# Column sums of the modulation vectors: from four 128x128 TensorE transposes per group to VectorE block transposes and four small products per stage

## The reference, cut to what matters

```python
c_act = jax.nn.silu(c)                                  # (1, 1024)
for l in range(DEPTH):                                  # 2 layers
    mod = c_act @ w_ada[l] + b_ada[l]                   # (1, 6144), w_ada[l]: 1024 x 6144
    sh1, sc1, g1, sh2, sc2, g2 = jnp.split(mod, N_MOD, axis=-1)
    h = modulate(rmsnorm(x, norm1[l]), sh1, sc1)
    ...
    x = x + g1[:, None, :] * (merged @ w_out[l])
    h2 = modulate(rmsnorm(x, norm2[l]), sh2, sc2)
    ...
    x = x + g2[:, None, :] * ((jax.nn.silu(gate) * up) @ w_ffn_out[l])
```

## Time and profile before

| | |
|---|---|
| median of three executions | 1434.57 us (1430.73 to 1435.50) |
| the profiled execution | 1434.96 us, its span 1433.1 us |
| TensorE busy / weight loads | 98% / 92% of the span |
| VectorE busy | 80% |
| ScalarE busy | 58% |
| DMA queue of the weights | 71.0% of 16 engines |
| chain that ended last | TensorE 77%, VectorE 11%, ScalarE 6%, issue 3%, DMA 2% |

### The profile page before, as it was taken

How to read it: one execution, slowest core, us unless ns; L and a number is a source line. 1 busy time by engine, 2 the same in 40 slices (tenths; PEclk the granted TensorE clock), 3 DMA queues, 4 the chain that set the end, 5 groups by cost and what they waited for, 6 DMA issues and landing times.

```text
span 1433.1 us, 25543 instructions
## 1 busy us (share of the span) xinstructions
PE 1407.3 (98%) x10339; PEld 1312.1 (92%) x10339; DVE 1145.7 (80%) x1799; ACT 828.5 (58%) x1249; POOL 10.5 (1%) x21
## 2 busy tenths in 40 slices
PE   8999999999999999999999999999999999999997
PEld 7898888889888888889999999998899999999986
DVE  7898888889798888887778777777777787778763
ACT  6776776445776875343666555444446575554542
POOL 2000000000000000000000000000000000000000
PEclk9999999999999999999999999999999999999999
DMA  9643999985445999987854578798787556778662
GB/s 257 161 140 92 284 266 268 299 229 163 137 140 169 278 259 295 284 248 217 226 153 144 172 233 233 212 250 231 225 235 217 148 147 180 231 208 232 180 186 64
DMA packets 485364, 297.13 MB, mean 207 GB/s; under 512 B 14956, under 2 KB 455792, under 8 KB 485120
## 3 DMA queue, kind: packets, MB, share of 16 engines
q1 hardware_dynamic: 483728, 292.00, 71.0%
q0 software_dynamic: 704, 1.66, 0.4%
q10 hardware_dynamic: 816, 1.84, 0.3%
HBM read 289.43 MB, written 1.05 MB: 203 GB/s over the span
## 4 chain that ended last, share of the span: by engine, by line
PE 77%; DVE 11%; ACT 6%; issue 3%; DMA 2%; SPq 1%; DVEq 0%; ACTq 0%
PE acc L1928 12%; PE acc L1929 12%; PE acc L1930 12%; PE mx L1945 9%; PE acc L1945 8%; PE mx L1946 5%; DVE w_lo L1073 4%; PE acc L1946 4%; DVE ada_acc L1163 2%; ACT w_hi L577 2%; PE acc L1960 1%; PE acc L1961 1%; PE acc L1962 1%; DMA rotb<-projb 1%; PE mx L2363 1%
## 5 line engine op out<-in xcount | busy, mean ns | idle before, releaser
L1073 DVE TENSOR_TENSOR w_lo<-raw,w_hi 128x1024 fp32r<-128x1024 f32 x450 | 541.5, 1220 | 113.3 <-ACT w_hi L577 111.4
L577 ACT ACTIVATE w_hi<-raw 128x1024 fp32r<-128x1024 f32 x450 | 458.2, 1049 | 137.7 <-DMA raw<-in_w_in 83.5
L1928 PE MATMUL acc<-h,w_hi 128*128 128x258 f32 (+1 forms) x1776 | 508.6, 286 | 8.4 <-DVE projb L1591 3.4
L1929 PE MATMUL acc<-h,w_hi 128*128 128x258 f32 (+1 forms) x1776 | 503.7, 284 | 0.0
L1930 PE MATMUL acc<-h,w_lo 128*128 128x258 f32 (+1 forms) x1776 | 498.0, 280 | 0.0
L1928 PEld LDWEIGHTS acc<-h,w_hi 128*128 128x128 f32 x1776 | 335.0, 189 | 15.7 <-issue 4.8
L1930 PEld LDWEIGHTS acc<-h,w_lo 128*128 128x128 f32 x1776 | 338.3, 190 | 0.0
L1929 PEld LDWEIGHTS acc<-h,w_hi 128*128 128x128 f32 x1776 | 335.9, 189 | 2.6 <-issue 2.4
L1945 PE MATMUL mx<-u,w_hi 128*128 128x512 f32 x864 | 303.4, 396 | 0.1
L1946 PE MATMUL mx<-u,w_lo 128*128 128x256 f32 x864 | 240.8, 279 | 0.0
L1945 PEld LDWEIGHTS mx<-u,w_hi 128*128 128x128 f32 x864 | 162.0, 188 | 37.1 <-DVE u L1877 0.4
(11 more groups left out here) (294 smaller groups left out, 1649.1 us busy)
## 6 DMA issues: line engine op xcount, KB each, us to landing
raw<-in_w_in SPq DMA_DIRECT2D x132, 512.0 KB, 4.0
ada<-in_w_ada SPq DMA_DIRECT2D x96, 512.0 KB, 5.0
raw<-in_w_ffn_in SPq DMA_DIRECT2D x88, 512.0 KB, 4.9
raw<-in_w_up SPq DMA_DIRECT2D x64, 512.0 KB, 5.6
raw<-in_w_down SPq DMA_DIRECT2D x64, 512.0 KB, 5.9
raw<-in_w_out SPq DMA_DIRECT2D x32, 512.0 KB, 3.9
raw<-in_w_ffn_out SPq DMA_DIRECT2D x32, 512.0 KB, 4.2
raw<-in_w_ret_o SPq DMA_DIRECT2D x16, 512.0 KB, 3.8
```

The lines of the kernel that those rows point to most:

```text
L577: nc.scalar.activation(w_hi[:, n % NS], raw[:, n % NS], ACT.Copy).then_inc(hi_ready, 1)
L1073: V.tensor_tensor(w_lo[:, n % NS], raw[:, n % NS], w_hi[:, n % NS].bitcast(F32), ALU.subtract).then_inc(lo_ready, 1)
L1928: mm(outp, w_hi[:, i % NS, k], rhs[:, k, 0], start=k == 0, stop=False)
L1929: mm(outp, w_hi[:, i % NS, k], rhs[:, k, 1], start=False, stop=False)
```

## The change

For a group, directly after its eighth product, VectorE now turns `ada_acc` in blocks of 32x32 (`V.transpose`, 128x512 to 128x512) and sums each of the sixteen blocks along its rows into 16 columns of `ada_rows`. Block `(q, b)` of the turned tile holds column `32*b + j` in partition `32*q + j`, summed over the 32 partitions of quarter `q`. What is left is a sum over the four quarters. For it, TensorE does four small float32 products once per stage, after the stage's last group: a 128x32 matrix of four stacked identities (`ada_fold`) times four to 28 columns, each into another 32 partitions of `mx[:, 0]`. VectorE adds the bias of the whole stage in one operation.

```diff
@@ VectorE: products
-                o = ada_acc[:, g % 2]
+                o = ada_acc[:, 0]
-                    if g >= 2:
-                        dve.wait_ge(ada_col, g - 1)
+                    if g >= 1:
+                        dve.wait_ge(ada_row, g)
@@ VectorE: sums
-            def ada_columns(g):
-                dve.wait_ge(ada_col, g + 1)
-                ca.link(V.tensor_reduce(ada_part[:], mx[:, 0].rearrange("p (n k) -> p n k", n=4), AX, ALU.add))
-                V.tensor_tensor(modT[:, 4 * g:4 * g + 4], ada_part[:], vecT[:, V_BADA + 4 * g:V_BADA + 4 * g + 4],
-                                ALU.add).then_inc(ada_out, 1)
+            def ada_turned(stage, g):
+                dve.wait_ge(ada_sum, ADA_UNITS * (g + 1))
+                ca.link(V.transpose(ada_acc[:, 1], ada_acc[:, 0]))
+                V.tensor_reduce(ada_rows[:, g - ADA_PLAN[stage][0]].rearrange("p n m -> p (n m)"),
+                                ada_acc[:, 1].rearrange("p (b k) -> p b k", b=16), AX, ALU.add).then_inc(ada_row, 1)
+            def ada_columns(stage):
+                g, n, at = ADA_PLAN[stage]
+                dve.wait_ge(ada_col, ADA_STAGES.index(stage) + 1)
+                V.tensor_tensor(modT[:, 4 * g:4 * (g + n)], mx[:, 0, 0:4 * n], vecT[:, V_BADA + 4 * g:V_BADA + 4 * (g + n)],
+                                ALU.add).then_inc(ada_out, n)
@@ VectorE: beside the MLP of A and beside F
                     for q in tiles.get(p, ()):
                         ada_product(q)
-                    if p in columns:
-                        ada_columns(columns[p])
+                        if q % 8 == 7:
+                            ada_turned(stage, q // 8)
+                    if p == ada_end(stage, 6):
+                        ada_columns(stage)
@@ VectorE: at the start, in rest_of_vectors
+                boot.done(V.tensor_reduce(ada_fold[:], ident.rearrange("p (a k) -> p k a", a=4), AX, ALU.add))
@@ VectorE: stage P
                 ada_product(8 * g0 + 7)
                 to_sbuf(8, 9)
+                ada_turned(("P", l), g0)
...
                 lo_upto(p0 + 20)
-                ada_columns(g0 + 0)
                 rope2(3)
...
                 to_sbuf(22)
+                ada_turned(("P", l), g0 + 1)
                 decayed(1)
                 to_sbuf(23)
-                ada_columns(g0 + 1)
+                ada_columns(("P", l))
@@ TensorE
-            def ada_sums(g):
-                pe.wait_ge(ada_sum, ADA_UNITS * (g + 1))
-                if g >= 1:
-                    pe.wait_ge(ada_out, g)
-                for n in range(4):
-                    ins = nc.tensor.transpose(mx[:, 0, n * P:(n + 1) * P], ada_acc[:, g % 2, n * P:(n + 1) * P], ident)
+            def ada_sums(stage):
+                g, n, at = ADA_PLAN[stage]
+                pe.wait_ge(ada_row, g + n)
+                for m in range(4):
+                    ins = mm(mx[32 * m:32 * (m + 1), 0, 0:4 * n], ada_fold[:], ada_rows[:, 0:n, :, m], start=True, stop=True)
                 ins.then_inc(ada_col, 1)
@@ TensorE: stage P (the call for the first group, after slab 12, is gone; the other stays before slab 25)
-                pe.wait_ge(ada_out, g0 + 1)
+                pe.wait_ge(n_var, l * 2 + 5)
                 ret_scores(0)
...
-                ada_sums(g0 + 1)
+                ada_sums(("P", l))
@@ TensorE: beside the MLP of A and beside F
-                    if p in sums:
-                        ada_sums(sums[p])
+                    if p == ada_end(("A", l), 4):
+                        ada_sums(("A", l))
```

More of the change, by code:

```diff
@@ L121, in ada_sums_at, with ada_end @@
     return {at(8 * i + 7) + later: g0 + i for i in range(n)}
+ADA_STAGES = (("A", 0), ("A", 1), ("P", 0), ("F", 0), ("P", 1), ("F", 1))
+def ada_end(stage, later):
+    g0, n, at = ADA_PLAN[stage]
+    return at(8 * n - 1) + later
 ADA_DONE = (0, 0, 7, 7, 14, 16, 20, 22, 24)
@@ L243, in program @@
         head_eps = sb("head_eps", [P, 1])
-        ada_part = sb("ada_part", [P, 4])
+        ada_fold = sb("ada_fold", [P, 32])
+        ada_rows = sb("ada_rows", [P, 7, 4, 4])
         few = sb("few", [P, 16])
@@ L343, in program @@
         ada_landed = [sem(f"ada_landed{j}") for j in range(3)]
[L344 removed]
+        ada_sum = sem("ada_sum"); ada_row = sem("ada_row"); ada_col = sem("ada_col"); ada_out = sem("ada_out")
         s_con = sem("s_con"); s_con2 = sem("s_con2"); s_x = [sem(f"s_x{n}") for n in range(2)]
@@ L1167, in ada_product @@
                     ca.done(ins)
-            def ada_columns(g):
-                dve.wait_ge(ada_col, g + 1)
-                ca.link(V.tensor_reduce(ada_part[:], mx[:, 0].rearrange("p (n k) -> p n k", n=4), AX, ALU.add))
-                V.tensor_tensor(modT[:, 4 * g:4 * g + 4], ada_part[:], vecT[:, V_BADA + 4 * g:V_BADA + 4 * g + 4],
-                                ALU.add).then_inc(ada_out, 1)
+            def ada_turned(stage, g):
[8 more added lines that the diff above has]
+                                ALU.add).then_inc(ada_out, n)
             def beside(stage):
-                tiles, columns = ada_tiles(stage), ada_sums_at(stage, 6)
+                tiles = ada_tiles(stage)
                 def work(p):
@@ L2293, in _ @@
                 up_slab(3)
-                sums = ada_sums_at(("A", l), 4)
                 def ada_after(p):
-                    if p in sums:
-                        ada_sums(sums[p])
+                    if p == ada_end(("A", l), 4):
+                        ada_sums(("A", l))
                 pe.wait_ge(n_var, l * 2 + 2)
@@ L2420, in _ @@
                 g0 = ADA_PLAN["P", l][0]
[L2421 to L2424, removed]
+                project(0, 1, 2, 3, 4, 5, 6, 7, 8, 9, 10, 11, 12, 13, 14, 15, 16)
                 values2(0)
                 project(17, 18)
-                pe.wait_ge(ada_out, g0 + 1)
+                pe.wait_ge(n_var, l * 2 + 5)
                 ret_scores(0)
@@ L2497, in _ @@
                 out_slab(7)
-                sums = ada_sums_at(("F", l), 4)
                 def ada_after(p):
-                    if p in sums:
-                        ada_sums(sums[p])
+                    if p == ada_end(("F", l), 4):
+                        ada_sums(("F", l))
                 for s in range(FFN_IN):
```

## The result

The changed kernel takes **1441.06 us** (median of 4 runs, 1440.10 to 1442.22), the kernel before 1434.45 us in 4 runs (1430.73 to 1435.5). The ratio is **1.0054** (95% interval 1.0037 to 1.0070): slower, by 6.6 us between the medians, and the whole interval lies above the 0.3% from which the forecast spoke of slower. The forecast was 1439.4 us, 1430.5 to 1446.0, with a chance of 0.47 on slower. The profiled execution took 1440.1 us (span 1438.2, mean granted clock 0.993); before it was 1434.96 us (span 1433.1, clock 0.997).

A forecast was written before the change was run, and what follows sets the result against it. VectorE's closed loop with ScalarE, not the 98% busy TensorE, was taken to bound A0, A1 and part of F: 1.8 + 1.6 + 2.4 - 0.3 - 0.6 = +4.9 us, giving 1439.4 us, range 1430.5 to 1446.

The forecast's parts named there:

- The bound: In A0, A1 and F's gate and up part, VectorE and ScalarE turn in a closed loop that sets the stage's end.
- 1.8 and 1.6 in the forecast: Last drains of A0 and A1: VectorE's added turnings less removed sums make them 1.8 and 1.6 us later.
- The turning: VectorE, per group: transpose (0.68 us) plus dependent row sum add 1.44 us, 0.64 us net of the old sum and bias.
- The third rival: The transpose passes its data twice, 1.23 us each, in A0, A1 and F of layer 0: 1446.6 us, chance 0.13.
- the sum at the start: The one 128-column sum at the kernel's start: under 0.3 us, taken as nothing.
- The place of the wait in A0 and A1: TensorE was to stand longer for VectorE at the first slab after A0 and A1.
- The step: A0's down part: TensorE, relieved of seven groups, only gets earlier to where it waits for VectorE; last drain +1.8 us.
- its own sign: Forecast wrong if TensorE's waits after A0, after A1 and at F of layer 0's first down bank are not longer.
- another of its signs: Forecast wrong if VectorE has idle time in the loops beyond the 1.9 us after each drain.
- a wait of "over 3 us": F of layer 0, first down bank: TensorE's step grows from 0.35 us to over 3 us.
- P: Both P stages: turnings fall within VectorE's waits, so TensorE gains 0.3 us each; without that cover, up to 1.44 us cost.
- The small products: Four narrow float32 TensorE products per stage cost 0.53 us, 0.27 if tiles run together, 1.05 without overlap; 3.2 us over six stages.

The follow-up runs named there:

- Experiment 4: Kernel before with one of a group's four TensorE transposes, VectorE's row sum reading that piece four times: 1431.07 us, ratio 0.9981.
- experiment 3: Kernel after without VectorE's 24 block transposes, row sums reading the unturned accumulator, TensorE's work unchanged: 1428.39 us, ratio 0.9956.
- experiment 2: Kernel after with eight unused 128x256 products ahead of each of TensorE's three waits, to keep the clock up: 1435.3 us, ratio 1.0007.
- Experiment 1: Kernel after with A0's and A1's small products moved behind the last down slab and the bias behind the last drain: 1441.52 us, ratio 1.0047.
- e6: Kernel before with VectorE's queued modulation products issued ahead of its wait for ScalarE after each drain: 1431.86 us, ratio 0.9986.
- e7: Kernel after with VectorE's queued modulation products issued ahead of its wait for ScalarE after each drain: 1422.73 us, ratio 0.9932.

## Why the prediction was right, and where its terms were not

**The bound: right.** VectorE's closed loop with ScalarE sets the ends of A0, A1 and F's gate and up part. Experiment 4 takes TensorE's work away and A0's MLP with the projections stays; experiment 3 takes VectorE's away and the time falls. With the clock kept (experiment 2), VectorE's last drain comes later against the start of the stage's MLP by 2.1 us in A0 and 1.6 us in A1, against 1.8 and 1.6 in the forecast, and F of layer 0 is 2.0 us longer, against 2.4. For A0, experiment 2's row and below it that of before, whose MLPs start at 140.62 and 141.19:

```profile
328.10 0.42 DVE L1595 TENSOR_TENSOR xT<-ru,xT 128x256 f32<-128x256 f32 x1
```
```profile
326.58 0.42 DVE L1574 TENSOR_TENSOR xT<-ru,xT 128x256 f32<-128x256 f32 x1
```

**The turning: right.** 1.46 us against 1.44. The transposition takes 0.710 us for 0.68, above the 0.63 us from which the forecast had the kernel slower by 0.3%. The third rival, two passes at 1.23 us, is out. The rule that the transposing mode sustains one element per cycle per lane, from the Trainium skill (Vector Engine (DVE) Microarchitecture Reference, The reshape front-end and per-opcode configuration), fits here: 0.710 us beside the row sum's 0.686 at as many columns. VectorE's busy time rose by 14.6 us for 13: the longer transposition is 0.7 of the difference. The rest is the sum at the start (0.39 us, where I had said under 0.3) and small ones.

**The place of the wait in A0 and A1: wrong.** The step said that TensorE "only gets earlier to where it waits for VectorE", and named the first slab after A0 and A1. By its own sign the forecast was wrong there: that wait did not grow (0.49 us in both kernels behind A0, 0.49 for 1.32 behind A1), and the 1.08 us of VectorE's idle time ahead of the last drain was another of its signs. The small products themselves wait for VectorE's turning. VectorE's modulation work has little lead over TensorE: in the kernel before the last modulation product of A0 ended at 315.05, and TensorE came for it at 316.1, with 1 us to spare; relieved of seven groups and with VectorE's turning between, it comes 3.5 us too early. I had priced these products as work and had not asked what they wait for. By itself the place costs little. Experiment 1 puts the wait where I had it and takes the same time.

**The clock: not foreseen.** Each of the three waits of some 3.5 us is followed by 3.4 us at the lower level, within the windows of some 4 us above. It costs 1.5 us each time. In the forecast there is a wait of "over 3 us" at 981.87, but no price behind it. With the clock kept, A0 and the projections behind it are at +2.1 us (forecast +1.8), and that is the turning's own cost there.

**P: too dear, partly by chance.** With the clock kept, the two rows of A1 and F in the table are together 4.0 us under the forecast (-0.9 for +1.3, +0.3 for +2.1). In P the kernel before stood for VectorE twice (TensorE's timeline):

```profile
674.15 0.39 PE L1928 MATMUL acc<-h,w_hi 128*128 128x258 f32 x1 [2.53 <-DVE projb L1591]
...
1066.71 0.39 PE L1928 MATMUL acc<-h,w_hi 128*128 128x258 f32 x1 [0.90 <-DVE projb L1591]
```

Whoever comes later waits less: 0.56 us and none in experiment 2, so that 2.9 of the 4.0 us are there. I had not looked at these two rows. But the projections of the two P also differ between kernels that have the same code there: 147.4 and 144.2 us before, 144.3 and 147.0 us in e6. They follow the waits: in e6 it is the second P that has a long one (2.17 us at 1063.24). How much of it the change brings, and how much is one execution's, stays open.

**The small products: a little too dear.** Counted as the forecast counted the transposes, in e7, where nothing waits: the next wide product would have started at 311.48 (0.12 us after 311.36), and that of line 1976 comes at 312.13, 0.65 us later instead of 0.24. So they cost 0.41 us a stage, not 0.53, as much as one group of the old transposes; that is 0.5 us in the four stages in which the forecast's sum has them. Their own part is the 0.22 us from 311.57 to 311.79 for eight records, where six products of 64 columns took 0.80. That fits the table of the Trainium skill (TensorEngine Tiling (Array Packing), Tiling Modes; that different tiles can run in parallel stands there under Key Properties), by which four tiles of 128x32 run together. The rest, about 0.1 us ahead of them and 0.1 us behind, is there too, and kept the sum from the lower bound of 0.27 us.

**The sum.** Without the clock the span is at +0.3 us for +4.9: 2.9 us by the waits in P, 0.5 by the small products, 0.6 before A0's MLP, 0.6 in small differences. In the kernel after, the clock adds 4.5 us, the projections and P 1.0 us, and A0's MLP starts 0.7 us earlier than in experiment 2: +5.1. So the number was right by luck, because what was too dear and what was missing (4.5 us of clock) cancel. The medians differ by 6.6 us, 1.7 more than the forecast.

## What to carry to other kernels

When an engine is relieved of work, ask of every instruction that is left, and of the new ones above all, what it waits for and how far behind the producer runs; a relieved TensorE comes to its waits earlier, and a wait of some microseconds can be paid a second time in the clock (here 1.5 us for each of three). In a closed loop of two engines, work queued behind the wait for the other one adds to the loop, and ahead of it most of it disappears in the idle time (here a product of 0.75 us took 0.85 us off the idle time). Here the order and the change needed each other: alone the order brought 2.0 us and the change lost 6.6, and together they brought 9.7. A sum that comes out right is no proof of its terms: compare stage by stage.

## What the runs showed that was not expected

After waits of TensorE of 3.5 us the granted clock was 0.58 to 0.60 over the next 4 us, but the length of the wait alone does not order the cases. After 2.17 us of idle time in experiment 1 it was 0.63, and after 2.17 us in e6 (P of layer 1, at 1063.24) it was 0.62 over the next 4.5 us. The kernel before has a wait of 2.53 us, and in its windows around it, the wait and the 3.9 us behind, the clock stays at 1.00:

```profile
671.30:674.10 2.80, 0.33 (x3) 0.12 (x1) 2.80 (x5) 0.00 (x0) 0.00 (x0) 1.00 0.65 201
674.10:678.00 3.90, 3.85 (x32) 3.85 (x33) 3.83 (x8) 0.00 (x0) 0.00 (x0) 1.00 0.69 190
```

What decides between these cases is open. Eight useless products in each of three waits showed no cost and were worth 5.8 us (experiment 2), which makes them a cheap test for a suspected loss of clock.
